# Gate and up products of a diffusion block in seven quadrant products instead of eight, with a rebuilt passage from the first layer norm

## The reference

```python
x = layer_norm(ALPHA * x + g1 * m, ln1_g, ln1_b)
h = x * (1 + sc2) + sh2
gate, up = jnp.split(h @ w_gu, 2, axis=-1)
f = (jax.nn.silu(gate) * up) @ w_down
x = layer_norm(ALPHA * x + g2 * f, ln2_g, ln2_b)
```

## Time and profile before

| | us |
|---|---|
| median of 3 runs | 3020.45 (3017.72 to 3021.79) |
| the profiled run | 3021.84 |
| its span, first to last instruction | 3020.0 |
| TensorE busy | 2849.6 (94%) |
| VectorE, ScalarE, GpSimd busy | 796.7, 754.5, 616.0 |
| mean granted TensorE clock | 0.973 |

### The profile page before, as it was taken

How to read it: one execution, slowest core, us unless ns; L and a number is a source line. 1 busy time by engine, 2 the same in 40 slices (tenths; PEclk the granted TensorE clock), 3 DMA queues, 4 the chain that set the end, 5 groups by cost and what they waited for, 6 DMA issues and landing times.

```text
span 3020.0 us, 37685 instructions
## 1 busy us (share of the span) xinstructions
PE 2849.6 (94%) x17296; PEld 2571.9 (85%) x17296; DVE 796.7 (26%) x863; ACT 754.5 (25%) x727; POOL 616.0 (20%) x139
## 2 busy tenths in 40 slices
PE   5898999999969958999999999999999999999995
PEld 3577878789958848999999999999999988888884
DVE  4222232236636535000000000000000135344445
ACT  5222323232221163111111111111111232323233
POOL 0000000000000002333333333333333333333331
PEclk8899999999989978999999999999999999999998
DMA  9864655521364311222222222222222555554542
GB/s 334 308 214 152 206 195 195 194 91 64 111 221 135 101 56 61 83 84 92 83 90 86 83 96 81 85 96 79 89 92 79 180 199 176 180 185 171 188 160 109
DMA packets 147730, 414.00 MB, mean 137 GB/s; under 512 B 7772, under 2 KB 10212, under 8 KB 129652
## 3 DMA queue, kind: packets, MB, share of 16 engines
q1 hardware_dynamic: 145268, 406.35, 38.8%
q10 hardware_dynamic: 2304, 5.24, 0.5%
HBM read 382.96 MB, written 28.61 MB: 136 GB/s over the span
## 4 chain that ended last, share of the span: by engine, by line
PE 89%; DVE 4%; ACT 3%; DMA 3%; issue 1%; SPq 0%; ACTq 0%; DVEq 0%
PE ps L1416 41%; PE ps L1635 7%; PE ps L1633 7%; PE ps L1634 7%; PE ps L1359 5%; PE ps L1360 4%; PE ps L1361 4%; PE ps L1421 4%; PE ps L1341 3%; PE ps L1571 2%; PE ps L1572 2%; PE ps L1573 2%; DMA low<-w_ada 1%; ACT low L884 1%; DMA low<-mixed_scratch 1%
## 5 line engine op out<-in xcount | busy, mean ns | idle before, releaser
L654 POOL TENSOR_TENSOR w_lo<-raw_w,w_hi 128x2048 fp32r<-128x2048 f32 x132 | 613.9, 4651 | 1726.8 <-ACT w_hi L673 1726.8
L673 ACT ACTIVATE w_hi<-raw_w 128x2048 fp32r<-128x2048 f32 x181 | 346.9, 1916 | 1609.4 <-PE ps L1416 1040.2
L1416 PE MATMUL ps<-x_hi,w_hi 128*128 128x320 f32 x2816 | 643.3, 310 | 4.7 <-DVE x_lo L1242 4.7
L1416 PE MATMUL ps<-x_hi,w_lo 128*128 128x320 f32 x2816 | 643.1, 310 | 0.0
L1416 PE MATMUL ps<-x_lo,w_hi 128*128 128x320 f32 x2816 | 643.1, 310 | 0.0
L1416 PEld LDWEIGHTS ps<-x_hi,w_hi 128*128 128x128 f32 x2816 | 471.5, 188 | 4.9 <-DVE x_lo L1242 4.9
L1416 PEld LDWEIGHTS ps<-x_hi,w_lo 128*128 128x128 f32 x2816 | 471.4, 188 | 0.0
L1416 PEld LDWEIGHTS ps<-x_lo,w_hi 128*128 128x128 f32 x2816 | 471.3, 188 | 0.0
L1359 PE MATMUL ps<-x_hi,w_hi 128*128 128x320 f32 x1056 | 343.6, 325 | 5.4 <-DVE x_lo L1001 3.8
L1635 PE MATMUL ps<-w_hi,x_lo 128*128 128x512 f32 x880 | 342.6, 389 | 0.0
L1633 PE MATMUL ps<-w_hi,x_hi 128*128 128x512 f32 x880 | 342.6, 389 | 0.0
(11 more groups left out here) (147 smaller groups left out, 2033.8 us busy)
## 6 DMA issues: line engine op xcount, KB each, us to landing
raw_w<-w_gu_b SPq DMA_DIRECT2D x88, 1024.0 KB, 5.2
low<-w_ada SPq DMA_DIRECT2D x60, 1024.0 KB, 5.4
low<-hidden_scratch SPq DMA_DIRECT2D x44, 1280.0 KB, 6.0
raw_w<-w_down SPq DMA_DIRECT2D x44, 1024.0 KB, 5.1
raw_w<-w_in_b SPq DMA_DIRECT2D x33, 1024.0 KB, 7.3
high<-w_ada SPq DMA_DIRECT2D x22, 1024.0 KB, 5.3
raw_w<-w_out SPq DMA_DIRECT2D x16, 1024.0 KB, 5.0
first_ring<-w_ada SPq DMA_DIRECT2D x14, 1024.0 KB, 9.3
```

Of the source, the lines that this page charges most:

```text
L654: nc.gpsimd.tensor_tensor(w_lo[:, s, :], raw_w[:, s, :], w_hi[:, s, :].bitcast(F32), ALU.subtract).then_inc(split_done, 1)
L673: nc.scalar.activation(w_hi[:, s, :], raw_w[:, s, :], ACT.Copy).then_inc(w_hi_done, 1)
L1416: ins = mm(ps[:, banks + half, 0:HALF], w, x[:, k, half * HALF:(half + 1) * HALF], start=begin, stop=end)
```

## The change

The tokens are cut into two halves of 320, the inner dimension into two halves of 1024, and gate and up are the two halves of the output. The eight products of quadrants become seven, in Winograd's form of Strassen's scheme. Of the activations there are seven versions (`B11`, `B21`, `B22`, `T2`, `T3`, `T4`, `T1`; the T are differences), formed once by VectorE. Of the weights each block needs the four loaded quadrants and S1 to S4, formed by GpSimd in float32, four additions of 128 x 1024. Each of seven weight operands is rounded by ScalarE and its rest made by VectorE, three products ahead. VectorE and ScalarE add the seven products together out of PSUM (`post`).

Around it: the first norm's deviation is now a square root and a reciprocal; the normed rows are stored to DRAM (`normed_scratch`) because the T4 and T1 versions take the place of `u_acc`, and are loaded back when the last gate product is done; gain and shift of the norm are applied to them by VectorE in the seventh unit of each `nb` of the down product; the down product's five row vectors per `nb` come in one slot (three rows in two slots before).

```diff
+HK = KT // 2
+VER = HK * HALF
+QUAD = HK * P
+B11, B21, B22, T2, T3, T4, T1 = range(7)
+SLOT_AFTER = (B21, T2, B22, T3)
+N_PROD = 7 * FB
+A11, A12, A21, A22, S1 = range(5)
+W_OF = (A11, A12, A12, A11, A21, A22, S1)
...
+    def weight(part, n):
+        s = (n + 2) % 4
+        return w_slots[part][:, QUAD * s:QUAD * s + QUAD]
...
+        def load_quad(b, q):
+            unit, half = 2 * b + q // 2, q % 2
+            if b:
+                sp.wait_ge(prod_split, 7 * (b - 1) + (4, 3, 5, 6)[q])
...
+        for b in range(FB):
+            pool.wait_ge(quad_in[A21], 16 * (b + 1))
+            pool.wait_ge(quad_in[A22], 16 * (b + 1))
+            if b:
+                pool.wait_ge(prod_split, 7 * b)
...
+            nc.gpsimd.tensor_tensor(quad(S1), quad(A21), quad(A22), ALU.add).then_inc(s1_formed, 1)
+            pool.wait_ge(quad_in[A11], 16 * (b + 1))
+            pool.wait_ge(s1_formed, b + 1)
+            nc.gpsimd.tensor_tensor(quad(A21), quad(A11), quad(A21), ALU.subtract).then_inc(s3_formed, 1)
+            pool.wait_ge(prod_split, 7 * b + 1)
+            pool.wait_ge(s3_formed, b + 1)
+            nc.gpsimd.tensor_tensor(quad(A11), quad(S1), quad(A11), ALU.subtract).then_inc(s2_formed, 1)
+            pool.wait_ge(prod_split, 7 * b + 2)
+            pool.wait_ge(s2_formed, b + 1)
+            nc.gpsimd.tensor_tensor(quad(A12), quad(A12), quad(A11), ALU.subtract).then_inc(s4_formed, 1)
...
+        for n in range(N_PROD):
+            v = n % 7
+            pe.wait_ge(prod_split, n + 1)
+            bank_free(n)
+            for k in range(HK):
...
+                mm(prod_bank(n), wh, version(v, 0, k), start=k == 0, stop=False)
+                mm(prod_bank(n), wh, version(v, 1, k), start=False, stop=False)
+                ins = mm(prod_bank(n), wl, version(v, 0, k), start=False, stop=k == HK - 1)
+            ins.then_inc(prod_done, 1)
...
+        sp.wait_ge(prod_done, N_PROD)
+        sp.wait_ge(xn_out, 16 * TT)
+        sp.dma_start(u_acc, xn_d.rearrange("t p c -> p t c")).then_inc(xn_in, 16)
```

More of the change, by code:

```diff
@@ L891, in halves, with prod_round @@
[L891 to L902, removed]
+        def prod_round(n):
+            b, i = divmod(n, 7)
+            if n < 4:
+                act.wait_ge(unit_used, FU - 1 if n < 2 else FU)
+            else:
+                act.wait_ge(prod_done, n - 3)
+            if i < 2:
+                act.wait_ge(quad_in[i], 16 * (b + 1))
+            elif i == 2:
+                act.wait_ge(s4_formed, b + 1)
+            elif i == 3:
+                act.wait_ge(s2_formed, b + 1)
+            elif i == 4:
+                act.wait_ge(s3_formed, b + 1)
+            elif i == 5:
+                act.wait_ge(quad_in[A22], 16 * (b + 1))
+            else:
+                act.wait_ge(s1_formed, b + 1)
+            nc.scalar.activation(weight(0, n), quad(W_OF[i]), ACT.Copy).then_inc(prod_hi, 1)
@@ new lines, in _ @@
+        act.wait_ge(folded, 5)
+        act.wait_ge(unit_used, FU)
+        for k in range(HK):
+            fold_low(k, 0, h21, h21_ready)
+        act.wait_ge(h21_ready, HK)
+        round_version(whole(B21, 0), h21)
+        for k in range(HK):
+            fold_low(k, 1, h22, h22_ready)
+        act.wait_ge(h22_ready, HK)
+        round_version(whole(B22, 0), h22)
+        prod_round(2)
+        prod_round(3)
+        act.wait_ge(t_formed, 3)
+        round_version(whole(T2, 0), raw_version(T2))
@@ L1233, in _ @@
[L1233 to L1243, removed]
@@ new lines, in version_rest, with difference @@
+        def version_rest(out, src, hi, n):
+            dve.wait_ge(ver_hi, n)
+            nc.vector.tensor_tensor(out, src, hi.bitcast(F32), ALU.subtract).then_inc(ver_split, 1)
+        def difference(out, a, b):
+            nc.vector.tensor_tensor(out, a, b, ALU.subtract).then_inc(t_formed, 1)
+        dve.wait_ge(folded, 5)
+        for k in range(HK):
+            fold_high(k, 0, h11, h11_ready)
+        for c in range(2):
+            part = slice(c * VER // 2, (c + 1) * VER // 2)
+            version_rest(whole(B11, 1)[:, part], h11[:, part], whole(B11, 0)[:, part], c + 1)
@@ new lines, in _ @@
+        dve.wait_ge(unit_used, FU)
+        for k in range(HK):
+            fold_high(k, 1, h12, h12_ready)
+        dve.wait_ge(h12_ready, HK)
+        dve.wait_ge(turned2, 4 * HK)
+        dve.wait_ge(xn_out, 16 * TT)
+        difference(raw_version(T1), by_token(h12), by_token(h11))
+        version_rest(whole(B21, 1), h21, whole(B21, 0), 3)
+        dve.wait_ge(h22_ready, HK)
+        difference(raw_version(T3), h22, h12)
+        dve.wait_ge(t_formed, 1)
+        difference(by_token(raw_version(T2)), by_token(h22), raw_version(T1))
@@ L1270, in _ @@
+        for n in range(N_PROD + 1):
+            if n:
+                post(n - 1)
+            if 7 <= n + 3 < N_PROD:
+                prod_rest(n + 3)
+            if n == N_PROD - 2:
+                hid_rest(0)
         hid_rest(1)
-        hidden(FB - 1)
+        finish(FB - 1)
         stat2 = lo(D_RAW + 2 * DG * T, 24 * TT).rearrange("p (t c) -> p t c", t=TT)
@@ L1407, in _ @@
         main_part(1, 3)
-        def three_passes(s, k, banks, first, last):
-            wh = w_hi[:, s, k * P:(k + 1) * P]
-            wl = w_lo[:, s, k * P:(k + 1) * P]
-            for w, x, begin, end in ((wh, x_hi, first, False), (wh, x_lo, False, False),
-                                     (wl, x_hi, False, last)):
-                for half in range(2):
-                    ins = mm(ps[:, banks + half, 0:HALF], w, x[:, k, half * HALF:(half + 1) * HALF],
-                             start=begin, stop=end)
-            return ins
         def pair_mm(x, n, c, w, rhs, start, stop, **kw):
@@ new lines, in _ @@
+        pe.wait_ge(ln1_normed, 3)
+        for k in range(HK):
+            if k == 3:
+                pe.wait_ge(out_evac, OUT_ACC)
+            if k >= 4:
+                pe.wait_ge(h11_ready, k - 3)
+            turn_half(TURN_A[k % 4], k, 0)
+        for k in range(HK):
+            if k >= 3:
+                pe.wait_ge(h21_ready, k - 2)
+            turn_half(TURN_B[k % 3], HK + k, 0)
+        pe.wait_ge(ln1_normed, TT)
+        for k in range(HK):
+            if k < 4:
+                pe.wait_ge(h11_ready, k + 5)
+            else:
+                pe.wait_ge(h12_ready, k - 3)
+            turn_half(TURN_A[k % 4], k, 1)
```

478 lines of the change are left out of this document (333 added, 145 removed).

## The result

The changed kernel takes 2876.15 us (median of 4 runs, 2874.6 to 2878.37) against 3019.31 for the kernel before, a ratio of 0.9525 (95% interval 0.9511 to 0.9539). The forecast was 2870 in a range of 2848 to 2894. In a later set of runs the same kernel took 2882.23 (2876.98 to 2885.23), 0.9544 of before; its profiled execution reached the passage 9.7 us later, in stages ahead of the passage. Differences of a few microseconds between sets are therefore read from the traces.

The account below looks back on a forecast made before the run. TensorE alone was taken to set the gate and up stage. Products -154.9, passage -15.5, down product's start +18.8 and tail +1 sum to -150.6 on a span of 3020.0: 2869.4, forecast 2870 us, range 2848 to 2894.

Parts of the forecast that it names:

- The products: Gate and up stage: 168 matmuls a block instead of 192, 1056 removed at 0.1467 us, saving 154.9 us.
- Do the weights arrive in time?: Gate and up blocks: weights ready using 14.1 of 21.1 us, slack 7.0, or 2.1 with every lock; cost nothing.
- The rival with unfed blocks: Gate and up stage: GpSimd's and VectorE's lock stretches the weights' chain, 22 to 65 us more, 2892 to 2935; chance 0.13.
- The passage: From first layer norm to gate stage: product 9 starts at 1168.5, TensorE never waits afterwards, -15.5 us.
- The start of the down product: First unit waits 1 us; third unit's loads stand behind rows and reload, stall 15.2, clock 2.6: +18.8 us in all.
- Tail: Before the last products: five reciprocals, each with a handoff, +1 us, bounds 0 to 3.
- The hidden reload: Start of the down product: transfers of one queue overlap more, so the reload is hidden, 2852 us; chance 0.12.
- Slow reads of T4 and T1: Gate stage: operands in runs of 64 columns read slowly; from 1.7 us on each of 88 products no gain; chance 0.03.
- the slower case: Gate stage: GpSimd's addition of 1024 columns costs what 2048 do, 4.65 us, giving 3180 us; chance 0.04.

Follow-up runs that it names:

- the eighth product: The changed kernel with the matmuls of each block's seventh product issued a second time into the same bank: 3024.27 us, 1.0013 of the kernel before.
- the doubled T4: The changed kernel with the difference T4 in the passage formed twice on VectorE, same result: 2882.39 us in one run.
- the reordered first loads: The changed kernel with rows and reload late, first hidden group loaded before first down weights, third unit's loads before last hidden store: 2857.14 us, 0.9458.

## Why the prediction was right, and where it was not

- **The products.** Right, in mechanism and size: 154.9 us forecast, 154.3 by the eighth product within the stage.
- **Do the weights arrive in time?** The answer held (1.0 us of waiting in the stage), the reasoning did not. The step "S1 may start once the last product of the block before is split" failed: S1 waited for a load in 37 of 44 blocks (A22's is the last that it needs). I had priced a path open at both ends and left out the load of 5.6 us and the rests that must pass in order before it. Closed, the path is a loop of about 24.5 us beside TensorE's 24.64. Where I saw 7.0 us of room, or 2.1 with every lock, there is almost none: 2.6 us more in it cost 111 us. That the time stayed in the range is luck: a loop 0.6 us longer would have stood some 0.45 us above TensorE's block, by estimate 43 x 0.45 = 19 us more and past 2894. The rival with unfed blocks was nearer than its chance said, mainly through the load and the rests; the lock's part in the loop is 0.8 us a turn.
- **The passage.** -15.5 forecast, -14.7 by the last gate product (169.6 - 154.9). The nearness is in part errors that cancel. Product 9 started at 1165.70, 2.8 us ahead of the forecast, and the stage behind it took 3.4 us more than 299 x 3.52: 1.6 for slow matmuls behind that wait, 1.0 for the wait in the stage, the rest for a few slow matmuls later. The forecast that from there TensorE never waits was nearly so. Inside, the five tile turns ended 3 us early (1091.3 against 1094.4) and VectorE's line began 2 us late (1118.12 against 1116). VectorE's ten large operations and five weight rests run from 1118.12 to 1151.37, 33.3 us against 34.8; the doubled T4 shows that this line sets the end.
- **The start of the down product.** The mechanism was right, the sizes short. The rows were issued 14.0 us after the last gate product (2235.68), not 7: two of VectorE's last small operations met GpSimd's weight rests (320 columns took 4.34 and 4.89 us, where 0.48 is usual for the second), and the last store went out at 2233.10. The group landed 25.6 us after the rows (forecast 26.6). The wait was 17.4 instead of 15.2, the first unit's 2.75 instead of 1, and the slow matmuls were paid twice, 1.7 and 2.3 us, in place of 2.6 once: 24.2 in all against 18.8. This term carries nearly all of the 6.4 us by which the saving fell short (144.2 against 150.6).
- **Tail.** 1.0 us, as forecast.
- **The rivals.** The hidden reload is refuted by its removal. Slow reads of T4 and T1 are refuted by 309 ns in both groups. GpSimd's addition of 1024 columns takes 2.41 us, so the slower case fell with it.

What stays open: why the first hidden group lands earlier in some executions than in others, and with it whether the reordered first loads gain any time.

## What to carry to other kernels

A rule that frees a buffer closes a loop: follow it once all the way round, loads and in-order neighbours included, before comparing it with the engine that sets the pace. A path that hides under one engine with a fraction of a microsecond to spare per block looks free in the profile until the next change; doubling an instruction on it that leaves the result the same shows the room at once. The mean distance between turns does not show it, because the pacing engine sets that mean. When a large transfer is put on a queue, ask which load behind it is needed first.

## What the runs showed of the hardware

- Half the bytes did not land sooner: loads of 512 KB took 5.6 us from issue in the median, the 1024 KB units of the kernel before 5.2. Both are medians of loads that stand behind others on SP's queue; no run here takes size and queue apart.
- GpSimd's sum or difference of 1024 columns took 2.39 us at the least, and of 2048 4.59. The one of 8 columns took 1.00 us in the median but 0.205 at the least; as with 1024 columns (3.21 and 2.39), the 0.8 between is time in which VectorE kept it out. What is left lies on one line, about 0.2 us and 2.15 ns a column (an estimate from these three).
- That VectorE and GpSimd exclude each other hits short operations hardest. One product of 320 columns with both inputs in SBUF (L1540) took 1.18 us in the mean of 41 and 4.34 at the worst; another of the same shape (L1506) took 0.48 in the median and 4.89 at the worst. The sums of 320 columns with one input in PSUM took 0.47 to 0.49 throughout.
